# Rounding the values' weights ahead of the first keys' rotation copies, and giving the last norm's products two operands

## The chip, the cores and the metric

The kernel runs on one core of a Trainium2 chip. A core has five engines with instruction queues of their own: TensorE (PE: matmuls, and their weight loads, which the profile lists as PEld), VectorE (DVE), ScalarE (ACT), GpSimd (POOL) and SyncE (SP), which here only starts transfers. They are ordered among each other by semaphores alone. The metric is the time on the device of one execution, in microseconds (us); lower is better.

## The reference

Two layers of a transformer block over 512 tokens of width 1024, then a last norm. What matters here:

```python
def rms_norm(x, g):
    y = x * lax.rsqrt(jnp.mean(x * x, axis=-1, keepdims=True) + EPS)
    return y * g

for l in range(2):
    xn = rms_norm(x, attn_norm[l])
    (nsa_q, kv_c, kv_s, kv_w, nsa_g, cq, ckv, k_rope_raw, gate_a, gate_b) = split_cols(xn @ w_in[l])
    o_a = nsa_attention(nsa_q, kv_c, kv_s, kv_w, ...)    # rope() on queries and on the three keys
    o_b = mla_attention(cq, ckv, k_rope_raw, ...)
    merged = sigmoid(gate_a) * (o_a @ nsa_w_o[l]) + sigmoid(gate_b) * (o_b @ mla_w_o[l])
    x = x + merged @ w_out[l]
    hn = rms_norm(x, mlp_norm[l])
    x = x + jnp.square(jax.nn.relu(hn @ w_up[l])) @ w_down[l]
return rms_norm(x, final_norm)
```

## The kernel before

Activations are held transposed: `x` is 8 rows of 128 features by 512 tokens, row m being `x[:, m, :]`. Every operand of a matmul is split into a rounded part ("hi") and the rest ("lo"), and a product is three matmuls: hi by hi, hi by lo, lo by hi (lines 1375 to 1377; for the values' units 1426, 1428 and 1429). One layer is a `Fori` loop body that is written once and runs twice (l = 0 and 1).

**Weights** come in units of 128x1024 numbers (512 KB). SP loads a unit into one of two `stage` buffers, ScalarE writes its hi part (`split_hi`, line 599), and VectorE (`split_lo`, line 927) or GpSimd (`split_lo`, line 492) writes the lo part into one of two `wsplit` slots. The hi part of a unit waits for its transfer and for TensorE to have finished the unit two before it, which used the same slot. The first units of a layer are, in TensorE's order (`PREFIX`): KC (the first keys, 24 matmuls of 512 columns), VC, KS, V0 (first half of the values' unit pair, 48 matmuls of 256 columns), KW, V1, Q0, and more. GpSimd writes the lo part of V0; VectorE those of the others near it.

**Rotation** (rope) of item r, in the order of `ROPED` (KC is 0, KS is 1, KW is 2): VectorE multiplies the product tile by the cosines (`cosines`, line 977); ScalarE copies the tile with its quarters exchanged, in four instructions of 32 partitions (`swap`, line 635); VectorE multiplies that copy by the sines (line 981) and adds (line 989, both in `rotated`). What follows on ScalarE and VectorE is in written order. After KC's rotation come `copies(0)` (ScalarE, lines 670 and 671, four instructions), `blocks(0)` (VectorE, line 1009), `blocks_hi(0)` (ScalarE, line 676), and `swap(1)`. Then the hi part of V1, `rotated(1)` on VectorE, `k_hi(0)` (ScalarE, line 649, four instructions), `copies(1)`, `blocks(1)` on VectorE, `cosines(2)`, and only behind that VectorE's `split_lo` of Q0.

**ScalarE's queue** at the start of a layer: hi part of VC, `root`, hi part of KS, `spread`, `swap(0)`, hi part of V0, `copies(0)`.

**Norms.** For each row m ScalarE writes the square (line 605; row 0's goes to F[:, 2, :], the others' in turn to F[:, 1, :] and F[:, 0, :], row 7's to F[:, 1, :]) and the hi part of the scaled row (line 606). VectorE's `norm_sum` adds the square to the running sum F[:, 2, :] (line 938) and writes the lo part of the row (line 931). When all eight are added, TensorE's `mean_square` multiplies the sum by ones (line 1395: four calls, which appear as eight matmuls of one column). ScalarE takes the root (line 610), VectorE the reciprocal. There are five norms, n = 0 to 4: before layer 1, inside it, between the layers (n = 2), inside layer 2, and the last (n = 4). The sum of row 7 of norms 0 and 2 stands at the end of the work ahead of the layer's loop body, or at the end of the body.

**The end.** After the last product TensorE transposes the scaled `x` (line 1772, 32 calls of 128x128): 22 of them stand ahead of `mean_square(4)`, the others behind it. Once the reciprocal is there, ScalarE and VectorE scale the transposed tiles and SP and GpSimd send them out.

Of the kernel before, what the change touches and what calls it, by code (L numbers as in the profile page):

```python
# [12 lines left out]
P = 128  # L13
L = 2
S = 512
D = 1024
KT = D // P
QT = S // P
# [138 lines left out]
ROPED = [("KC", 0), ("KS", 0), ("KW", 0), ("Q", 0), ("Q", 1), ("Q", 2), ("Q", 3)]  # L157

PR_ATTN, PR_MLP, PR_QN, PR_KVN, PR_PE, NPAR = 0, 8, 16, 18, 19, 51
# [42 lines left out]
def build(nc, units, units_n, params, x_in, tables, cf32, cmasks, gates_dram, out):  # L202
    ctx = ExitStack()
    with ctx:
        def sb(name, shape, dt):
            return ctx.enter_context(nc.sbuf_tensor(name, shape, dt))

        def bank(name):
            return ctx.enter_context(nc.psum_tensor(name, [P, 512], F32))
# [21 lines left out]
        F = sb("F", [P, 8, S], F32)  # L231
# [7 lines left out]
        ones = sb("ones", [P, P], F32)  # L239
        par_all = sb("par_all", [P, L * NPAR + KT], F32)  # L240
        par = sb("par", [P, NPAR], F32)
        nextgain = sb("nextgain", [P, KT], F32)
# [29 lines left out]
        SB = [bank("S0"), bank("S1")]  # L272
# [4 lines left out]
        def sems(*names):  # L277
            return [sem(n) for n in names]
# [13 lines left out]
        def wslot(u):  # L292
            return narrow[:, SN[u] % 2] if u in SN else wsplit[:, BN[u] % 2]
# [81 lines left out]
        s_sq, s_sqadd = sems("s_sq", "s_sqadd")  # L375
        s_eps, s_masks, s_maskrow = sems("s_eps", "s_masks", "s_maskrow")
        s_mstand = sem("s_mstand")
        s_ms, s_rms, s_rec, s_diag, s_spread, s_rs = sems("s_ms", "s_rms", "s_rec", "s_diag", "s_spread", "s_rs")
# [217 lines left out]
        def _(act):  # L596
            def split_hi(l, u, f=0):
                split_begins(act, l, u, f)
                act.activation(wslot(u)[:, 0, :], staged(u), ACT.Copy).then_inc(s_whin if u in SN else s_whi, 1)  # L599
# [12 lines left out]
            def spread(n):  # L612
                act.wait_ge(s_spread, n + 1)
                act.activation(rs[:, :], SB[0][:, :], ACT.Copy).then_inc(s_rs, 1)
# [10 lines left out]
            with act.Fori(0, L) as l:  # L625
                def emptied(t):
                    act.wait_ge(s_gfree, l * NG + (TILE[t] + 1 + GFREE0))
# [16 lines left out]
                def k_hi(br):  # L644
                    act.wait_ge(s_roped, l * 7 + (2 + br))
                    for gr in range(2):
                        k = F[64 * gr:64 * gr + 64, 4 + (br + 1) % 2, :]
                        for hf in range(2):
                            ins = act.activation(KN[64 * hf:64 * hf + 64, br, gr, 0, :], k, ACT.Copy)
                    ins.then_inc(s_rhi, 1)  # L650

                def v_hi():
                    act.wait_ge(s_rs, l * 2 + 1)
                    act.wait_ge(s_wused, l * NU + (UNIT["V", 1] + 1 + WUSED0))
                    for tt in range(QT):
                        src = SB[tt // 2][:, 256 * (tt % 2):256 * (tt % 2) + 256].rearrange("p (a n) -> p a n", n=HD)
                        dst = VN[:, tt, :, :, 0:HD].rearrange("p b g n -> p (b g) n")
                        ins = act.activation(dst, src, ACT.Copy, scale=rc[:, 0, tt:tt + 1])
                    ins.then_inc(s_vhi, 1)

                def copies(kind):
                    if kind == 0:
                        act.wait_ge(s_roped, l * 7 + 1)
                        src = F[:, 4, :]
                    else:
                        emptied(("VC", 0))
                        act.wait_ge(s_tb, l * 2 + 1)
                        src = E[:, 0, :]
                    for gr in range(2):
                        act.activation(E[0:64, 1 + gr, :], src[64 * gr:64 * gr + 64, :], ACT.Copy)  # L670
                        ins = act.activation(E[64:128, 1 + gr, 0:S - 1], src[64 * gr:64 * gr + 64, 1:S], ACT.Copy)
                    ins.then_inc(s_cc, 1)

                def blocks_hi(kind):
                    act.wait_ge(s_tb, l * 2 + (kind + 1))
                    act.activation(TB[:, kind, :, 0, :], tbf.rearrange("p (j n) -> p j n", j=16), ACT.Copy)\
                        .then_inc(s_tbhi, 1)
# [121 lines left out]
                for u, item in enumerate(PREFIX):  # L799
                    name, i = item  # L800
                    if u in BN and item != ("GATE", FIRST_GATE - 1):
                        split_hi(l, BIG[BN[u] + 2])
                    if u == 0:
                        spread(l * 2)
                    if name == "VC":
                        copies(0)
                    if name == "KS":
                        blocks_hi(0)
                    if item == ("V", 0):
                        k_hi(0)  # L810
                        copies(1)
                    if name == "KW":
                        blocks_hi(1)
                    if item == ("V", 1):
                        v_hi()
                        k_hi(1)
                    if item == ("CQ", 0):
                        q_hi(0)
                    if item == ("CQ", 1):
                        q_hi(1)  # L820
                    if name == "CQ":
                        c_square(i)
                    if item == ("Q", 2):
                        c_root()
                    if name == "MISC":
                        q_hi(2)
                        swap_key()
                    if item == ("Q", 3):
                        nsa_gates()
                        hidden_copy(0)  # L830
                        hidden_tanh(0)
                    if item in ROPED:
                        swap(ROPED.index(item))
                    if item == ("GATE", 0):
                        hidden_hi(0)
                        split_hi(l, UNIT["W2K", 0])
                        q_hi(3)
                    if item == ("GATE", 2):
                        kc_hi()
                    if item == ("W1", 7):  # L840
                        hidden_copy(1)
                        hidden_tanh(1)
                    if name == "GATE":
                        gate_tanh(i)
                    for n in SMALL_AT.get(item, []):
                        split_hi(l, SMALL[n])
# [75 lines left out]
        def _(dve):  # L922
            chain = Chain(dve, s_dvec)

            def split_lo(l, u, f=0):
                split_rounded(dve, l, u, f)
                dve.tensor_tensor(wslot(u)[:, 1, :], staged(u), wslot(u)[:, 0, :], ALU.subtract)\  # L927
                    .then_inc(s_wlon[SN[u] % 2] if u in SN else s_wlo[BN[u] % 2], 1)

            def rest(out_ap, full, scale, hi):  # L930
                return dve.scalar_tensor_tensor(out_ap, full, scale, hi, ALU.mult, ALU.subtract)  # L931

            def norm_sum(n, m, gain):
                dve.wait_ge(s_sq, n * KT + (m + 1))
                if m > 0:
                    if m > 1:
                        dve.wait_ge(s_sqadd, n * KT + m)
                    dve.tensor_tensor(F[:, 2, :], F[:, 2, :], F[:, m % 2, :], ALU.add).then_inc(s_sqadd, 2 if m == 1 else 1)
                dve.wait_ge(s_xhi, n * KT + (m + 1))
                rest(xg[:, 1, m, :], x[:, m, :], gain, xg[:, 0, m, :]).then_inc(s_xlo, 1)  # L940

            def norm_diagonals(n):
                dve.wait_ge(s_rms, n + 1)
# [8 lines left out]
            dve.wait_ge(s_params, 16)  # L952
            split_lo(0, 0)
            for m in range(KT):
                norm_sum(0, m, par_all[:, PR_ATTN + m:PR_ATTN + m + 1])
            dve.wait_ge(s_const, 48)
            dve.tensor_copy(constb[:, :, :].rearrange("p c n -> p (c n)"), F[:, 4, 0:3 * P]).then_inc(s_masks, 1)
            with dve.Fori(0, L) as l:
# [236 lines left out]
                    dve.tensor_tensor(H[:, 1, m, :], F[:, 6 + m % 2, :], H[:, 0, m, :], ALU.subtract).then_inc(s_mglo, 1)  # L1195

                chain.restart()
                split_lo(l, 1)
                dve.wait_ge(s_xlo, l * 16 + 8)
                dve.tensor_copy(nextgain[:, :], par_all[:, bass.ds(l * NPAR + NPAR, KT)])  # L1200
# [160 lines left out]
                    up(f + 1)  # L1361
                for k in range(KT):
                    down(QUARTERS - 1, k, k < KT - 1)
                    norm_sum(l * 2 + 2, k, nextgain[:, k:k + 1])
            dve.wait_ge(s_rms, L * 2 + 1)
            dve.reciprocal(rc[:, 0, :], rc[:, 1, :]).then_inc(s_rec, 1)
            dve.wait_ge(s_rec, L * 2 + 1)
# [5 lines left out]
        def _(pe):  # L1373
# [18 lines left out]
            def mean_square(n):  # L1392
                pe.wait_ge(s_sqadd, n * KT + KT)
                for tt in range(QT):
                    ins = pe.matmul(SB[1][:, tt:tt + 1], F[:, 2, tt * P:(tt + 1) * P], ones[:, 0:1], start=True, stop=True)
                ins.then_inc(s_ms, 1)
# [371 lines left out]
            def turn_x(b, ms):  # L1768
# [4 lines left out]
                                       xs[m][:, (b % QT) * P:(b % QT) * P + P], ident)  # L1773
                return ins

            pe.wait_ge(s_gfree, L * NG + (GFREE0 - KT + 7))
            for b in range(4):
                turn_x(b, range(4)).then_inc(s_turned, 1)
            for b in range(4, 6):
                turn_x(b, range(4, 7))  # L1780
            mean_square(L * 2)
            for b in range(4, 6):
                turn_x(b, range(7, 8)).then_inc(s_turned, 1)
            pe.wait_ge(s_gfree, L * NG + GFREE0)
# [119 lines left out]
```

## Time and profile before

| what | value |
|---|---|
| median of 3 runs | 1550.94 us (1549.37 to 1550.97) |
| the profiled execution, whole | 1549.4 us |
| its span in the trace | 1547.5 us |
| PE busy | 1508.3 us, 97% of the span |
| PEld busy | 1260.6 us, 81% |
| DVE busy | 890.0 us, 58% |
| ACT busy | 723.9 us, 47% |
| POOL busy | 437.4 us, 28% |

The trace covers one execution, from its first to its last instruction; 1.9 us lie around it. A busy share says how much of the span an engine was computing. It doesn't say which engine is late at a given place: for that the waits and the timeline of a stretch are read.

### The profile page before, as it was taken

The numbers are of one execution on the slowest core, as the hardware profiler recorded it, in microseconds if no ns is written. First come the engines' busy times: TensorE is split into PE (matmuls) and PEld (weight loads), VectorE is DVE, ScalarE is ACT, GpSimd is POOL, SyncE is SP. The second block draws the span as 40 slices with busy tenths as digits, with TensorE's granted clock in tenths as the row PEclk, the third lists the DMA queues.
The fourth block names the chain that finished last, engine by engine and source line by source line (L and its number), as shares of the span: only waits on it lengthen the run. The fifth ranks groups of instructions, "written<-read, shape, count | busy, mean of one in ns | idle before, by whom it ended". The sixth has DMA issues, their size and how long they took to land.

```text
span 1547.5 us, 23290 instructions
## 1 busy us (share of the span) xinstructions
PE 1508.3 (97%) x7404; PEld 1260.6 (81%) x7404; DVE 890.0 (58%) x1537; ACT 723.9 (47%) x1316; POOL 437.4 (28%) x456
## 2 busy tenths in 40 slices
PE   6999999999999999999999999999999999999997
PEld 5888888888888888888888788787878888888886
DVE  6765755766654444535556757566675535354455
ACT  6753777874432222222366547777744212222233
POOL 1301666775010100101021036767730201010011
PEclk9999999999999999999999999999999999999999
DMA  5333212125222222322324422111352222223223
GB/s 194 109 130 123 91 67 76 42 89 173 100 95 96 95 95 95 96 95 99 105 69 136 150 82 83 56 69 57 96 176 96 96 95 96 101 94 104 95 95 109
DMA packets 43273, 155.56 MB, mean 101 GB/s; under 512 B 5312, under 2 KB 5312, under 8 KB 43168
## 3 DMA queue, kind: packets, MB, share of 16 engines
q1 hardware_dynamic: 36864, 133.19, 25.6%
q0 software_dynamic: 5728, 19.00, 3.6%
q10 hardware_dynamic: 576, 2.10, 0.4%
q8 instruction: 51, 0.84, 0.2%
q14 instruction: 54, 0.44, 0.1%
HBM read 143.78 MB, written 10.49 MB: 100 GB/s over the span
## 4 chain that ended last, share of the span: by engine, by line
PE 80%; issue 9%; DVE 3%; POOL 3%; ACT 2%; DMA 1%; POOLq 0%; DVEq 0%; ACTq 0%
PE G L1375 13%; PE G L1377 13%; PE G L1376 13%; PE O L1377 8%; PE O L1376 8%; PE O L1375 8%; PE O L1648 3%; PE T L1624 3%; PE S L1599 2%; PE T L1375 1%; PE T L1376 1%; PE T L1377 1%; POOL wsplit L492 1%; PE O L1450 1%; DVE F L1326 1%
## 5 line engine op out<-in xcount | busy, mean ns | idle before, releaser
L599 ACT ACTIVATE wsplit<-stage 128x1024 fp32r<-128x1024 f32 x229 | 242.4, 1058 | 608.9 <-PE G L1377 280.4
L927 DVE TENSOR_TENSOR wsplit<-stage,wsplit 128x1024 fp32r<-128x1024 f32 x181 | 264.3, 1460 | 70.7 <-ACT wsplit L599 64.1
L1375 PE MATMUL G<-xg,wsplit 128*128 128x512 f32 x592 | 238.6, 403 | 12.4 <-DVE xg L931 10.8
L585 POOL TENSOR_TENSOR F<-Y 128x512 f32<-128x512 f32 x64 | 68.4, 1069 | 637.3 <-DVE Y L1343 637.3
L1377 PE MATMUL G<-xg,wsplit 128*128 128x512 f32 x592 | 231.6, 391 | 0.0
L1376 PE MATMUL G<-xg,wsplit 128*128 128x512 f32 x592 | 231.6, 391 | 0.0
L492 POOL TENSOR_TENSOR wsplit<-stage,wsplit 128x1024 fp32r<-128x1024 f32 x48 | 116.1, 2419 | 138.3 <-ACT wsplit L599 137.8
L1134 DVE CUSTOM_DVE_ANT_0 F<-S,F 128x512 f32<-128x512 f32 x192 | 93.7, 488 | 101.6 <-PE S L1599 64.4
L1375 PEld LDWEIGHTS G<-xg,wsplit 128*128 128x128 f32 x592 | 111.6, 189 | 37.2 <-DVE xg L931 13.8
L754 ACT ACTIVATE F<-F,nmx 128x512 f32<-128x512 f32 x192 | 107.7, 561 | 64.9 <-DVE nmx L1134 63.1
L1377 PEld LDWEIGHTS G<-xg,wsplit 128*128 128x128 f32 x592 | 111.4, 188 | 24.4
L1376 PEld LDWEIGHTS G<-xg,wsplit 128*128 128x128 f32 x592 | 111.7, 189 | 20.7 <-issue 1.0
L1375 PE MATMUL G<-area,wsplit 128*128 128x512 f32 x320 | 124.7, 390 | 0.1
L1375 PE MATMUL O<-area,wsplit 128*128 128x512 f32 x320 | 124.5, 389 | 0.0
L1376 PE MATMUL G<-area,wsplit 128*128 128x512 f32 x320 | 124.5, 389 | 0.0
L1377 PE MATMUL O<-area,wsplit 128*128 128x512 f32 x320 | 124.5, 389 | 0.0
L1377 PE MATMUL G<-area,wsplit 128*128 128x512 f32 x320 | 124.5, 389 | 0.0
L1376 PE MATMUL O<-area,wsplit 128*128 128x512 f32 x320 | 124.5, 389 | 0.0
L1144 DVE TENSOR_TENSOR area_b<-T,area_b 128x512 fp32r<-128x512 f32 x192 | 92.8, 483 | 25.1 <-ACT area_b L749 22.3
L1375 PE MATMUL O<-xg,wsplit 128*128 128x512 f32 x256 | 99.6, 389 | 0.0
L1376 PE MATMUL O<-xg,wsplit 128*128 128x512 f32 x256 | 99.6, 389 | 0.0
L1377 PE MATMUL O<-xg,wsplit 128*128 128x512 f32 x256 | 99.6, 389 | 0.0
(286 smaller groups left out, 3001.9 us busy)
## 6 DMA issues: line engine op xcount, KB each, us to landing
stage<-units SPq DMA_DIRECT2D x230, 512.0 KB, 3.3
stage_n<-units_n SPq DMA_DIRECT2D x22, 512.0 KB, 3.3
gates<-Y POOLq DMA_DIRECT2D x32, 256.0 KB, 2.7
E<-gates POOLq DMA_DIRECT2D x24, 256.0 KB, 3.7
x<-x_in ACTq DMA_DIRECT2D x4, 512.0 KB, 7.1
F<-gates POOLq DMA_DIRECT2D x8, 256.0 KB, 3.8
rope<-tables POOLq DMA_DIRECT2D x1, 768.0 KB, 7.1
out<-F SPq DMA_DIRECT2D x3, 256.0 KB, 2.2
```

The costliest lines, as they stand in the source:

```text
L492: pool.tensor_tensor(wslot(u)[:, 1, :], staged(u), wslot(u)[:, 0, :], ALU.subtract)\
L585: pool.tensor_tensor(F[:, m % 2, :], Y[:, m % 2, :], Y[:, m % 2, :], ALU.mult)\
L599: act.activation(wslot(u)[:, 0, :], staged(u), ACT.Copy).then_inc(s_whin if u in SN else s_whi, 1)
L754: act.activation(prob(i, w), prob(i, w), ACT.Exp, bias=nmx[:, i % 4:i % 4 + 1], scale=-1.0, accum_out=sums[:, i % 4:i % 4 + 1]).then_inc(s ...
L927: dve.tensor_tensor(wslot(u)[:, 1, :], staged(u), wslot(u)[:, 0, :], ALU.subtract)\
L1134: dve.tensor_tensor_reduce(prob(i, w), score_tile(i), maskrow[:, S - w:S], -1.0, 1e38, ALU.add, ALU.min, nmx[:, i % 4:i % 4 + 1]).then_inc ...
L1144: dve.tensor_tensor(pt_view(slot, 1, qt), tp_view(j % 2, qt), pt_view(slot, 0, qt), ALU.subtract)\
L1375: pe.matmul(dst, a(0), b(0), start=first, stop=False)
L1376: pe.matmul(dst, a(0), b(1), start=False, stop=False)
L1377: return pe.matmul(dst, a(1), b(0), start=False, stop=last)
L1624: ins = pe.transpose(TP[j % 2][:, kt * P:(kt + 1) * P], prob(j, S)[:, kt * P:(kt + 1) * P], ident)
L1648: ins = pe.matmul(dst[:, kt * P:S], v, PT[:, slot, c, kt * S:(kt + 1) * S - kt * P], start=opens and c == 0, stop=closes(j) is not None an ...
```

## The change

Three edits. ScalarE's `swap(0)` moves from its place ahead of V0's hi part to the place right behind it. The running sum's last addition is taken out of `norm_sum`: for norms 0 and 2 it becomes the first instruction of the layer's body on VectorE, ahead of the lo part of VC and behind the lo part of row 7. For norm 4 the addition is dropped, and TensorE multiplies two operands by ones and accumulates them: the sum of seven rows, and the last row's square. Norms 1 and 3 keep `norm_sum` as it was.

```diff
 (ScalarE, in the loop over PREFIX)
                     if name == "VC":
+                        swap(0)
                         copies(0)
...
-                    if item in ROPED:
+                    if item in ROPED and u > 0:
                         swap(ROPED.index(item))
 (VectorE)
-            def norm_sum(n, m, gain):
+            def row_sum(n, m):
                 dve.wait_ge(s_sq, n * KT + (m + 1))
                 if m > 0:
                     if m > 1:
                         dve.wait_ge(s_sqadd, n * KT + m)
                     dve.tensor_tensor(F[:, 2, :], F[:, 2, :], F[:, m % 2, :], ALU.add).then_inc(s_sqadd, 2 if m == 1 else 1)
+
+            def row_lo(n, m, gain):
                 dve.wait_ge(s_xhi, n * KT + (m + 1))
                 rest(xg[:, 1, m, :], x[:, m, :], gain, xg[:, 0, m, :]).then_inc(s_xlo, 1)
+
+            def norm_sum(n, m, gain):
+                row_sum(n, m)
+                row_lo(n, m, gain)
...
             for m in range(KT):
-                norm_sum(0, m, par_all[:, PR_ATTN + m:PR_ATTN + m + 1])
+                if m < KT - 1:
+                    row_sum(0, m)
+                row_lo(0, m, par_all[:, PR_ATTN + m:PR_ATTN + m + 1])
...
                 chain.restart()
+                row_sum(l * 2, KT - 1)
                 split_lo(l, 1)
...
                     down(QUARTERS - 1, k, k < KT - 1)
-                    norm_sum(l * 2 + 2, k, nextgain[:, k:k + 1])
+                    if k < KT - 1:
+                        row_sum(l * 2 + 2, k)
+                    row_lo(l * 2 + 2, k, nextgain[:, k:k + 1])
 (TensorE, at the end)
+            def last_squares(src, first):
+                for tt in range(QT):
+                    ins = pe.matmul(SB[1][:, tt:tt + 1], src[:, tt * P:(tt + 1) * P], ones[:, 0:1],
+                                    start=first and tt == 0, stop=not first, skip_group_check=True)
+                return ins
...
                 turn_x(b, range(4, 7))
-            mean_square(L * 2)
+            pe.wait_ge(s_sqadd, L * 2 * KT + KT - 1)
+            last_squares(F[:, 2, :], True)
+            pe.wait_ge(s_sq, L * 2 * KT + KT)
+            last_squares(F[:, 1, :], False).then_inc(s_ms, 1)
             for b in range(4, 6):
```

## Rows read from the trace of the kernel before

**Rows 1.** Page, chain of work that ended last, shares by engine and line.
```profile
PE 80%; issue 9%; DVE 3%; POOL 3%; ACT 2%; DMA 1%; POOLq 0%; DVEq 0%; ACTq 0%
```
**Rows 2.** Waits of TensorE, whole span: total us, times, longest.
```profile
PE S L1426 <- POOL wsplit L492: 3.0, 2, 1.5
```
**Rows 3.** Timeline of TensorE, first 52 us: start, us, line, tiles, idle before.
```profile
26.38 0.39 PE L1377 MATMUL G<-xg,wsplit 128*128 128x512 f32 x1
...
33.70 0.36 PE L1426 MATMUL S<-wsplit,xg 128*128 128x256 f32 x1 [1.49 <-POOL wsplit L492]
...
51.38 0.49 PE L1375 MATMUL G<-xg,wsplit 128*128 128x512 f32 x1 [0.48 <-DVE wsplit L927]
```
**Rows 4.** Timeline of ScalarE, 27 to 46 us.
```profile
27.48 2.40 ACT L635 ACTIVATE F<-G 32x512 f32<-32x512 f32 x4 [2.16 <-DVE F L977]
29.90 1.06 ACT L599 ACTIVATE wsplit<-stage 128x1024 fp32r<-128x1024 f32 x1
31.36 0.63 ACT L670 ACTIVATE E<-F 64x512 f32<-64x512 f32 x1 [0.40 <-DVE F L989]
...
37.04 2.40 ACT L635 ACTIVATE F<-T 32x512 f32<-32x512 f32 x4
39.73 1.07 ACT L599 ACTIVATE wsplit<-stage 128x1024 fp32r<-128x1024 f32 x1 [0.29 <-PE S L1429]
40.91 2.56 ACT L649 ACTIVATE area<-F 64x512 fp32r<-64x512 f32 x4
...
45.43 0.63 ACT L671 ACTIVATE E<-E 64x511 f32<-64x511 f32 x1
```
**Rows 5.** Timeline of VectorE, 26 to 52 us.
```profile
26.75 0.69 DVE L977 TENSOR_TENSOR F<-G,Y 128x512 f32<-128x512 f32 x1
...
30.63 0.69 DVE L989 TENSOR_TENSOR F<-F 128x512 f32<-128x512 f32 x1
...
40.19 0.69 DVE L989 TENSOR_TENSOR F<-F 128x512 f32<-128x512 f32 x1
...
47.05 2.00 DVE L1009 TENSOR_TENSOR E<-E,par 128x496 f32<-128x496 f32 x1
...
49.57 1.68 DVE L927 TENSOR_TENSOR wsplit<-stage,wsplit 128x1024 fp32r<-128x1024 f32 x1
```
**Rows 6.** Timeline of GpSimd, the lo part of V0 in layer 1.
```profile
31.04 2.51 POOL L492 TENSOR_TENSOR wsplit<-stage,wsplit 128x1024 fp32r<-128x1024 f32 x1 [21.20 <-ACT wsplit L599]
```
**Rows 7.** Timeline of VectorE, row 7 of norm 0 and entry into layer 1.
```profile
17.09 0.68 DVE L938 TENSOR_TENSOR F<-F 128x512 f32<-128x512 f32 x1
17.69 0.75 DVE L931 SCALAR_TENSOR_TENSOR xg<-x,par_all,xg 128x512 fp32r<-128x512 f32 x1
...
18.62 1.22 DVE L927 TENSOR_TENSOR wsplit<-stage,wsplit 128x1024 fp32r<-128x1024 f32 x1
```
**Rows 8.** Timeline of TensorE, KC and the first matmul of VC, layer 1.
```profile
11.09 0.63 PE L1375 MATMUL G<-xg,wsplit 128*128 128x512 f32 x1
...
18.49 0.50 PE L1375 MATMUL G<-xg,wsplit 128*128 128x512 f32 x1 [0.30 <-DVE xg L931]
...
20.12 0.49 PE L1375 MATMUL G<-xg,wsplit 128*128 128x512 f32 x1
```
**Rows 9.** Timelines of VectorE and TensorE where layer 2 begins.
```profile
778.94 1.23 DVE L927 TENSOR_TENSOR wsplit<-stage,wsplit 128x1024 fp32r<-128x1024 f32 x1 [2.46 <-ACT wsplit L599]
...
780.29 0.49 PE L1375 MATMUL G<-xg,wsplit 128*128 128x512 f32 x1 [0.45 <-DVE wsplit L927]
```
**Rows 10.** DMA queues in 775 to 779.5 us: packets, MB, share.
```profile
q14 instruction: 4, 0.03, 2.6%
```
**Rows 11.** Timelines of VectorE, TensorE and ScalarE at the last norm.
```profile
1536.24 0.69 DVE L938 TENSOR_TENSOR F<-F 128x512 f32<-128x512 f32 x1 [0.78 <-ACT F L605]
...
1536.99 1.05 PE L1395 MATMUL S<-ones,F 128*128 128x1 f32 x8
...
1538.08 0.26 ACT L610 ACTIVATE rc<-S,small 128x4 f32<-128x4 f32 x1 [1.26 <-PE S L1395]
```

## The prediction on record

> **What bounds the kernel now.** I read the chain of work that ended last first. TensorE makes up 80% of it [rows 1], so a microsecond is won or lost only where TensorE stands idle, or at the two ends of the kernel. Next I read TensorE's waits. The wait for GpSimd's lo part of V0 appears twice, once a layer, 3.0 us in total [rows 2]: that is the wait which the moved `swap(0)` bears on. Then I read the timelines of the stretch, engine by engine, to see what comes late once that wait is gone. TensorE stands idle 1.49 us before V0, then works without a gap, and stands idle once more, 0.48 us, before Q0's first matmul at 51.38 [rows 3]. The reader should note that this second wait ends with VectorE's lo part of Q0, and ask what that in turn hangs on.
>
> It hangs on a chain through ScalarE and VectorE that begins with `swap(0)`. Link by link: cosines(0) end at 26.75 + 0.69 = 27.44 [rows 5]; swap(0) starts at 27.48 and ends at 29.88 [rows 4]; the two instructions of rotated(0) end at 30.63 + 0.69 = 31.32 [rows 5]; copies(0) start at 31.36, behind an idle 0.40 that this addition ends, and not V0's hi part, which was done at 29.90 + 1.06 = 30.96 [rows 4]. Copies, blocks(0), blocks_hi(0) and swap(1) follow. swap(1) runs from 37.04 to 39.44 [rows 4]. rotated(1) ends at 40.19 + 0.69 = 40.88 [rows 5] and k_hi(0) starts at 40.91, although ScalarE was free at 39.73 + 1.07 = 40.80 [rows 4]: the rotation was the later of the two. copies(1) end at 45.43 + 0.63 = 46.06 [rows 4]; blocks(1), stretched by a 2.00 us instruction, end at 49.05, cosines(2) follow, and the lo part of Q0 ends at 49.57 + 1.68 = 51.25 [rows 5]. TensorE starts at 51.38. Not one of these links waits for TensorE or for V0. A delay of swap(0) arrives whole at Q0.
>
> **The change, part one: swap(0) behind V0's hi part.** V0's hi part needs VC finished on TensorE: last matmul at 26.38 + 0.39 = 26.77 [rows 3]. With one semaphore's lag of about 0.04 (27.44 to 27.48 above) it starts at 26.81. It takes 1.06 and the next instruction follows 0.03 later: swap(0) starts at 27.90 instead of 27.48, **0.42 us late**. V0's lo part follows at 27.96 instead of 31.04 [rows 6] and ends near 30.4, ahead of the 32.21 (33.70 less 1.49) at which TensorE had finished KS. So the 1.49 us wait goes. But Q0 now starts 0.42 later than before, since its chain starts 0.42 later; the 1.49 us gained before V0 is spent waiting at Q0, where the idle grows from 0.48 to 0.48 + 1.49 + 0.42 = 2.4 us, or some 2.2 us and the rest before KW, whose lo part also moves back by 0.42. Behind Q0 all three engines are later by the same 0.42 and keep their distances. Layer 2 shows the same two waits in the same order, so I count it the same: 2 x 0.42 = **+0.84 us**. The bounds: nothing at all lost if a link has slack that I don't see (lower end 0), and 0.42 plus 0.15 a layer if rotated(0), starting at 30.33 while GpSimd still works on V0, is held up by it (upper end 1.14). I take 0.84, because every link shows its start within 0.04 us of the end before it.
>
> V0's transfer is no hindrance: SP can start it when VC's lo part is done (18.62 + 1.22 = 19.84 [rows 7]), seven microseconds ahead. SP's next transfer, V1's, starts about 3 us sooner, and nobody waited for it.
>
> **Part two: row 7's addition moved, norm 0.** VectorE now does the lo part of row 7 in place of the addition, at 17.09 and not 17.69 [rows 7], then the constants' cast, then the addition. TensorE's last three matmuls of KC waited for that lo part, 0.30 us at 18.49 [rows 8]. They start earlier, and mean_square with them. The next limit is the lo part of VC: the same instructions stand ahead of it in sum, so it still ends at 19.84, and VC can begin about 0.12 later (778.94 + 1.23 = 780.17, start 780.29 [rows 9]), at 19.96 in place of 20.12 [rows 8]. **-0.16 us.** Bounds: 0, and -0.30 if the whole wait were to come back.
>
> **Part two again, norm 2, where layer 2 begins.** Here the lo part of row 7 didn't wait for the addition but for ScalarE, so nothing comes earlier. The addition now stands behind the loop's jump, ahead of VC's lo part, and TensorE waited for just that lo part: 0.45 us at 780.29 [rows 9]. An addition takes 0.69 alone and 0.60 in a row of instructions (17.09 to 17.69 [rows 7]). The question is whether it fits into VectorE's idle 2.46 us before 778.94. The row names ScalarE's hi part as the releaser, but that unit's hi part began 1.6 us after ScalarE's own last work, and VectorE started 0.58 us after it ended, where 0.04 is usual. So VectorE itself wasn't back from the jump before 778.94, and the instruction queue's transfers run in this stretch [rows 10]. The addition then runs at about 778.94 and everything behind it is 0.61 later: **+0.61 us**, with bounds 0 (it fits into the idle time) and 0.8 (its two waits are worked out behind the jump too). The Trainium skill has a rule for this, in "Runtime: NRT & Kernel Launch", section "Instruction fetch mechanics": a taken branch to a page that isn't held makes the engine wait for a fetch before it goes on. By that rule the addition can't use the gap and costs its 0.6; by the releaser that the profile names it would cost nothing.
>
> **Part three, the last norm.** The addition of row 7 ends at 1536.24 + 0.69 = 1536.93, and the eight one-column matmuls begin at 1536.99 [rows 11]. Its removal looks like 0.69 us won. But TensorE was transposing without a gap up to 1536.98: no idle stands in front of that row. At most 0.12 us, the distance of one weight load, is won. What is added is a second set of eight. A set takes 1.05 us from first start to last end, with a last matmul of about 0.27, so (1.05 - 0.27) / 7 = 0.11 apart, 0.92 for eight. The first set isn't ready-made in idle time either; it stands behind the same transposes. So the root, released by the last of them at 1538.08 [rows 11], comes 0.92 - 0.12 = **+0.80 us** later, and behind it the reciprocal, the scaling and the output transfers, with nothing else to hide it. Bounds: 0.4, if the second set's loads overlap better, and 0.95.
>
> **Sum.** 0.84 - 0.16 + 0.61 + 0.80 = +2.1 us. The profiled execution took 1549.4 whole (span 1547.5 and 1.9 around it), so 1551.5 by it. The median shown is 1.54 above that execution: **1553.0 us**. The bounds add up to 0 - 0.30 + 0 + 0.4 = +0.1 and 1.14 + 0 + 0.8 + 0.95 = +2.9. The difference that a measurement of this kernel can tell from none is about 0.2%, 3.1 us. The forecast is 0.14% slower, inside it: no change.
>
> **Rivals.**
> *The wait at V0 is really won.* If a link of the chain to Q0 has slack of 2 us, both waits shrink: 2 x -1.49 - 0.16 + 0.61 + 0.80 = -1.7, 1549.2 us. For it speaks that this is the longest wait of the stretch; against it each link in rows 4 and 5. Chance 0.08.
> *The addition fits into the gap at the jump.* +1.5 in all, 1552.4 us. For it speaks the releaser in rows 9; against it the 0.58 us lag. Chance 0.15.
> *The longer idle time costs TensorE its clock; this one ends slower.* In the kernel's first matmuls, after 9.6 us of idleness, a matmul of 512 columns takes 0.63 [rows 8] against 0.39 later [rows 3], which are the levels of 1.2 and 2.4 GHz. After 1.49 us of idleness the clock was still at 2.4 GHz. The idle time before Q0 grows to 2.2 to 2.4 us, between the two. If the clock falls there, the price by the kernel's start, where about six matmuls went slow, is 6 x 0.24 = 1.4 us a layer: 2.1 + 2.8 = +4.9, 1555.8 us, 0.3% slower. It decides if as few as three matmuls go slow in each layer (0.7 a layer, 3.5 in all). "TensorE: Matmul & The Clock Gate", Part 1, in the Trainium skill says that idleness brings the lower clock back; no row here shows an idle time of this length, so it stays open which side of that rule it falls on. Chance 0.12.
> The forecast itself has 0.65.
>
> **How the numbers follow.** Faster by over 0.2% would need more than the first rival gives: 0.04, half of its chance, for unseen slack on top. Slower by over 0.2%: the clock's 0.12 and 0.04 for a sum at its upper end: 0.16. Within 0.2%: 0.80. The range runs from 1550.5, which holds the bound of +0.1 less the scatter of the three runs shown, to 1555.5, which leaves out the far half of the clock's case; the first rival lies outside it. The forecast's own range is 1551.0 to 1554.0.
>
> **What the profile of the changed kernel would show.** Right: no wait before V0; swap(0) starting 1.09 us behind the start of V0's hi part and 1.1 us behind the end of VC's last matmul; a wait of 2.2 us or more before Q0, still ended by VectorE's lo part; Q0 at about 51.38 - 0.16 + 0.42 = 51.64; at the layer's start an addition on VectorE at about 778.9 with 0.6 us more before VC; 16 one-column matmuls at the end and the root 0.8 us later, counted from the last product. Wrong: Q0 starting earlier than 51.2, matmuls of 0.63 us behind its wait, or the 16 taking no longer than the eight did.

## The result and the profile after

The changed kernel takes **1553.56 us** in the median of 11 executions (1550.27 to 1556.02), the kernel before 1550.36 in its 11 (1549.15 to 1552.08). The ratio is 1.002, with a 95% interval of 1.001 to 1.0029: slower by 0.2%, some 3 us. The forecast was 1553.0 us in 1550.5 to 1555.5, and 0.14% slower. The second measurement of the same kernel (e13 below) gives 1.0021 (1.0012 to 1.003).

The profiled execution took 1555.03 us, with a span of 1553.2. That is 5.7 us above the span of before, and nearly twice what the medians differ by, so it can't be read as the price of the change before it is taken apart. First come TensorE's waits over the whole span (total us, times, longest us), with those left out that hardly moved:

```profile
PE G L1387 <- DVE wsplit L928: 4.6, 4, 2.2
...
PE S L1407 <- DVE F L939: 0.7, 1, 0.7
...
PE T L1387 <- DVE wsplit L928: 0.3, 2, 0.2
```

The wait for V0 [rows 2] is gone, and the waits for VectorE's lo parts took its place: two of 2.1 to 2.2 us before Q0, and two of 0.16 before KW (two of 0.16 before VC are in the first row as well). A new one, for the moved addition, stands where layer 2 begins. The timelines of layer 1 show the chain, beginning with TensorE (the first row is VC, the second KW, the third Q0):

```profile
20.07 0.50 PE L1387 MATMUL G<-xg,wsplit 128*128 128x512 f32 x1 [0.16 <-DVE wsplit L928]
...
38.06 0.51 PE L1387 MATMUL T<-xg,wsplit 128*128 128x512 f32 x1 [0.16 <-DVE wsplit L928]
...
51.70 0.49 PE L1387 MATMUL G<-xg,wsplit 128*128 128x512 f32 x1 [2.12 <-DVE wsplit L928]
```

ScalarE and VectorE in the same stretch:

```profile
26.75 1.06 ACT L599 ACTIVATE wsplit<-stage 128x1024 fp32r<-128x1024 f32 x1 [1.49 <-PE G L1389]
27.84 2.39 ACT L635 ACTIVATE F<-G 32x512 f32<-32x512 f32 x4
31.71 0.63 ACT L670 ACTIVATE E<-F 64x512 f32<-64x512 f32 x1 [1.48 <-DVE F L998]
...
41.27 2.56 ACT L649 ACTIVATE area<-F 64x512 fp32r<-64x512 f32 x4 [0.40 <-DVE F L998]
```
```profile
49.93 1.65 DVE L928 TENSOR_TENSOR wsplit<-stage,wsplit 128x1024 fp32r<-128x1024 f32 x1
```

Counted from VC's first matmul, which takes out what differs ahead of it, swap(0) starts 7.77 us later where it was 7.36 [rows 4, 8], and Q0 31.63 us later where it was 31.26 [rows 3, 8]. The delay of 0.41 passes down the links (copies(0) 0.40, k_hi(0) 0.41, the lo part of Q0 0.41) and is 0.37 at TensorE. V0's earlier start is all in the wait.

Where layer 2 begins, first row 7's lo part on VectorE in the kernel before, then VectorE and TensorE in the changed kernel:

```profile
775.72 0.75 DVE L931 SCALAR_TENSOR_TENSOR xg<-x,nextgain,xg 128x512 fp32r<-128x512 f32 x1
```
```profile
778.84 0.75 DVE L932 SCALAR_TENSOR_TENSOR xg<-x,nextgain,xg 128x512 fp32r<-128x512 f32 x1 [1.39 <-ACT xg L606]
782.19 0.69 DVE L939 TENSOR_TENSOR F<-F 128x512 f32<-128x512 f32 x1 [2.59 <-issue]
782.80 1.22 DVE L928 TENSOR_TENSOR wsplit<-stage,wsplit 128x1024 fp32r<-128x1024 f32 x1
```
```profile
782.94 1.05 PE L1407 MATMUL S<-ones,F 128*128 128x1 f32 x8 [0.73 <-DVE F L939]
784.15 0.49 PE L1387 MATMUL G<-xg,wsplit 128*128 128x512 f32 x1 [0.16 <-DVE wsplit L928]
784.48 0.39 PE L1388 MATMUL G<-xg,wsplit 128*128 128x512 f32 x1
784.71 0.46 PE L1389 MATMUL G<-xg,wsplit 128*128 128x512 f32 x1
784.97 0.63 PE L1387 MATMUL G<-xg,wsplit 128*128 128x512 f32 x1
```

The addition waits out the jump as well: its idle time of 2.59 us is now put down to "issue" and to no other engine, where in [rows 9] the profile had named ScalarE. The square that it adds had been written at 778.19, so it had nothing else to wait for. Then comes something that no price of the forecast's sum holds. From 784.97 on a matmul takes 0.63 us instead of 0.39: TensorE's clock has fallen from 2.4 to 1.2 GHz (the granted clock from 785 to 788 us is 0.50). Eight matmuls later it is back. They took 3.4 us where eight at the usual distance of 0.23 take 1.84, so this fall costs 1.5. There is another in this execution, near 88 us, that begins within the 24 one-column matmuls of the latent norms:

```profile
86.43 3.15 PE L1529 MATMUL T<-ones,csq 128*128 128x1 f32 x24
...
91.29 0.63 PE L1387 MATMUL T<-xg,wsplit 128*128 128x512 f32 x1
```

The busy times of 88 to 92 us (PE, PEld, DVE, ACT, POOL; then the granted clock, the DMA share, GB/s) give 0.57 for the clock:

```profile
88.00:92.00 4.00, 4.00 (x21) 3.90 (x21) 0.94 (x1) 2.33 (x6) 0.00 (x0) 0.57 0.04 14
```

The last norm: the last product in the kernel before, then TensorE and ScalarE in the changed kernel:

```profile
1534.35 0.39 PE L1377 MATMUL O<-area,wsplit 128*128 128x512 f32 x1
```
```profile
1539.26 0.39 PE L1389 MATMUL O<-area,wsplit 128*128 128x512 f32 x1
...
1541.89 1.84 PE L1790 MATMUL S<-ones,F 128*128 128x1 f32 x16
```
```profile
1543.77 0.26 ACT L610 ACTIVATE rc<-S,small 128x4 f32<-128x4 f32 x1 [2.04 <-PE S L1790]
```

From the last product's start to the root it is 4.51 us. Before it was 1538.08 less 1534.35, 3.73 us: 0.78 more.

**How executions are compared below.** Each execution lists its mean granted clock. In the kernel before it takes values from 0.995 to 0.998, and the time goes with it: the 92 executions in the first three rows of the table below average 1552.2, 1550.4, 1549.3 and 1548.4 us at 0.995, 0.996, 0.997 and 0.998. So beside the medians I compare executions with the same mean clock, as long as the kernels end alike (the clock also falls behind the last matmul, and a kernel with another end shifts the mean by that). The changed kernel ends a little otherwise: its clock is low for the last 7.1 us of its profile and 6.8 of e13's, against 5.8 before. That lowers its mean by 0.0003 to 0.0004, so a difference at equal clock is good to some 0.4 us there.

### The profile page after: what moved, and what is told of

The parts are those of the page before. It is cut to its first block, busy times and chain, and to the rows that moved or that the text cites. A ratio compares the mean times of both kernels' runs of the same rounds, so it can differ in the third digit from the quotient of the medians.

```text
span 1553.2 us, 23306 instructions
## 1 busy us (share of the span) xinstructions
PE 1512.6 (97%) x7412; PEld 1265.1 (81%) x7412; DVE 888.5 (57%) x1536; ACT 723.9 (47%) x1316; POOL 437.1 (28%) x456
## 4 chain that ended last, share of the span: by engine, by line
PE 83%; issue 5%; DVE 5%; ACT 3%; POOL 3%; DMA 1%; DVEq 0%; POOLq 0%; ACTq 0%
PE G L1387 14%; PE G L1389 13%; PE G L1388 13%; PE O L1389 8%; PE O L1388 8%; PE O L1387 8%; PE O L1660 3%; PE T L1636 3%; PE S L1611 2%; PE T L1387 2%; PE T L1389 1%; PE T L1388 1%; POOL wsplit L492 1%; PE O L1462 1%; ACT F L635 1%
```

## The experiments

| kernel | median us (n) | ratio, 95% | mean us at clock 0.998 (n) | executions at 0.995 or less |
|---|---|---|---|---|
| before, beside e1 to e4 | 1550.39 (33) | | 1548.5 (8) | 1 |
| before, beside e6 to e10 | 1549.98 (27) | | 1548.3 (7) | 1 |
| before, beside e11 to e14 | 1550.21 (32) | | 1548.4 (2) | 0 |
| changed | 1553.56 (11) | 1.002, 1.001 to 1.0029 | 1550.3 (1) | 4 |
| changed again, e13 | 1553.34 (11) | 1.0021, 1.0012 to 1.003 | 1550.8 (3) | 4 |
| e1, swap(0) moved | 1552.11 (11) | 1.0014, 1.0004 to 1.0023 | 1549.4 (3) | 5 |
| e14, e1 with the wait filled | 1550.55 (11) | 1.0002, 0.9993 to 1.0011 | 1549.1 (3) | 1 |
| e2, additions moved | 1551.78 (11) | 1.0015, 1.0006 to 1.0024 | 1550.7 (3) | 4 |
| e3, two operands at the end | 1551.08 (11) | 1.0007, 0.9998 to 1.0017 | 1549.5 (1) | 2 |
| e4, swap moved, Q0 early | 1549.84 (11) | 0.9998, 0.9989 to 1.0007 | none | 1 |
| e6, two operands, early | 1549.85 (11) | 1.0001, 0.9992 to 1.001 | ends otherwise | 1 |
| e8, squares spread | 1550.95 (11) | 1.0008, 0.9999 to 1.0018 | 1550.9 (7) | 0 |
| e9, changed, squares spread | 1556.42 (5) | 1.0042, 1.0028 to 1.0056 | none | 3 |
| e10, e4, e6 and e8 together | 1549.67 (11) | 1.0001, 0.9992 to 1.001 | ends otherwise | 0 |
| e11, e4 and e6 together | 1549.13 (11) | 0.9993, 0.9984 to 1.0002 | ends otherwise | 0 |
| e12, e11 and CQ0 early | 1546.33 (10) | 0.9977, 0.9968 to 0.9987 | ends otherwise | 0 |

### The parts one by one: e1, e2, e3

**e1** is the kernel before with the diff's two edits of `swap` and nothing else.

> Only ScalarE's swap(0) is moved behind V0's hi part; the norms are as in the kernel before. Theory (the chain from swap(0) to Q0's lo part has no slack): no wait before V0, a wait of 2.1 to 2.4 us before Q0, Q0's first matmul 0.4 us later than before in both layers, 0.8 us slower in all (ratio about 1.0005, same). Rival (the wait at V0 is really won): 3 us faster, ratio 0.998. Rival (the longer idle time before Q0 costs TensorE its clock): matmuls of 0.63 us right behind that wait, 1.4 us a layer more, ratio about 1.002. Second rival on the clock, from the changed kernel's trace: it falls elsewhere, at the start of layer 2, and then this kernel shows no slow matmuls there, because it has no added wait at that place.

Its profiled execution shows the waits of layer 1 that the theory names, and no slow matmuls behind them:

```profile
PE G L1376 <- DVE wsplit L928: 2.1, 1, 2.1
...
PE T L1376 <- DVE wsplit L928: 0.2, 1, 0.2
```

At a mean clock of 0.998 it takes 1549.4 against 1548.5 us, 0.9 us more; the forecast's term was 0.84. The rival in which V0's wait is really won falls. But the median is 1.7 us up, and 5 of 11 executions have a clock of 0.995 or less, where the kernel before has 2 in 92. The rival on the clock isn't refuted by a single profile without a fall.

**e2** moves the additions of norms 0 and 2; that of norm 4 stands behind the loop:

```diff
+                row_sum(l * 2, KT - 1)
                 split_lo(l, 1)
...
+            row_sum(L * 2, KT - 1)
             dve.wait_ge(s_rms, L * 2 + 1)
```

> Only the additions of row 7 of norms 0 and 2 are moved to the start of the layer's body; that of norm 4 stands behind the loop, and the last products are as before. Theory: 0.1 to 0.2 us earlier in layer 1, 0.6 us later in layer 2, 0.45 us slower in all. If the clock falls at the start of layer 2 because of the wait that this edit adds ahead of the one-column matmuls, eight matmuls of 0.63 us or so follow in the first tile of layer 2 and cost 1.6 us more: about 2 us slower, ratio 1.0013. Rival (the fall is chance or belongs to another edit): none of them here, ratio 1.0003.

It came out 2.2 us slower at equal clock (three executions; 1.4 in the median) and not 0.45. Two things that its forecast didn't price show in its profile. The first is its own end, TensorE and then VectorE:

```profile
1539.42 1.05 PE L1407 MATMUL S<-ones,F 128*128 128x1 f32 x8 [1.12 <-DVE F L938]
```
```profile
1538.01 0.75 DVE L931 SCALAR_TENSOR_TENSOR xg<-x,nextgain,xg 128x512 fp32r<-128x512 f32 x1 [1.39 <-ACT xg L606]
1538.68 0.68 DVE L938 TENSOR_TENSOR F<-F 128x512 f32<-128x512 f32 x1
```

The addition now stands behind row 7's lo part, which waits for ScalarE's hi part. VectorE shows no idle time at the loop's exit; the written order alone makes the addition late, and TensorE waits 1.12 us for it. The root comes 5.01 us behind the last product's start (1535.50 to 1540.51), where it was 3.73: 1.28 more. The second is the start of layer 2: from the start of row 7's lo part to VC's first matmul it is 5.52 us (776.80 to 782.32) against 4.57 (775.72 to 780.29), 0.95 more, of which 0.34 is a longer jump (VectorE idle 2.80 us where it was 2.46). With 0.15 won at norm 0, 1.28 + 0.95 - 0.15 makes 2.1 of the 2.2.

No fall of the clock stood at the start of layer 2 in its profile, though the same wait of 0.7 us did. So the fall at that place isn't certain in any one execution. And 4 of its 11 executions are at 0.995 or less although Q0's wait is as it was: the low executions don't come from that wait alone.

What the addition costs at the jump is read from the profiles: the same stretch is 5.31 us in the changed kernel and 5.33 in e13, 0.74 and 0.76 more than before. In e1, which doesn't touch this place, it is 4.89, because the jump took 0.3 longer there.

**e3** takes the two operands at the end alone. Row 7's sum goes into a row of its own, so that the sum of seven rows is still there for norm 4:

```diff
-                    dve.tensor_tensor(F[:, 2, :], F[:, 2, :], F[:, m % 2, :], ALU.add).then_inc(s_sqadd, 2 if m == 1 else 1)
+                    dve.tensor_tensor(F[:, 3 if apart else 2, :], F[:, 2, :], F[:, m % 2, :], ALU.add).then_inc(s_sqadd, 2 if m == 1 else 1)
...
-            mean_square(L * 2)
+            pe.wait_ge(s_sqadd, L * 2 * KT + KT - 1)
+            last_squares(F[:, 2, :], True)
+            pe.wait_ge(s_sq, L * 2 * KT + KT)
+            last_squares(F[:, 1, :], False).then_inc(s_ms, 1)
```

> Only the last norm takes two operands, at the same place in TensorE's queue as in the changed kernel. Row 7 of norms 0, 2 and 4 is still added where it was, but into a row of its own, which the products of norms 0 and 2 read. Theory: 16 one-column matmuls instead of 8, the root 0.8 us later counted from the last product, 0.8 us slower in all, nothing else changed. Rival (the addition that is gone from the path counts): 0 to 0.6 us faster.

The 16 matmuls take 1.84 us and the root comes 4.51 us behind the last product's start, as in the changed kernel: 0.78 more than before. The median is 0.7 us up, in an interval that just holds no change. The theory held in the profile, and the median fits it without telling it from no change.

### Is Q0's chain what swallows the gain: e4, e12

**e4** takes Q0's parts out of the chain's end:

```diff
                         k_hi(0)
+                        split_hi(l, UNIT["Q", 0])
                         copies(1)
...
                     if item == ("V", 0):
+                        split_lo(l, UNIT["Q", 0])
                         blocks(1)
```

> swap(0) moved as in e1, and Q0's hi part taken ahead of copies(1) on ScalarE, its lo part ahead of blocks(1) on VectorE. Theory (the 1.49 us won at V0 are lost at Q0 alone): both waits vanish, Q0 starts near 49.7 us instead of 51.4, about 1.7 to 1.9 us faster a layer as long as the tiles behind Q0 aren't late (they carry 1.1 us more of ScalarE's work ahead of them), 2 to 3.6 us faster in all, ratio 0.998. Rival (something else than Q0's weights holds TensorE there): no faster than the kernel before.

Half right. Q0's wait vanished, but a new one came a unit later, before CQ0:

```profile
56.48 0.49 PE L1378 MATMUL G<-xg,wsplit 128*128 128x512 f32 x1 [1.54 <-DVE wsplit L929]
```

Of up to 3.6 us it kept a few tenths: its executions at a clock of 0.997 average 1549.1, those of the kernel before beside them 1549.9 (two only), and all 18 of the kernel before 1549.3. So Q0's weights were what held TensorE, and behind them stand CQ0's.

**e12** is e11 (below) with CQ0's parts moved forward in the same way.

```diff
                     if name == "KW":
+                        split_hi(l, UNIT["CQ", 0])
                         blocks_hi(1)
...
+                        split_lo(l, UNIT["CQ", 0])
                         blocks_lo(1)
```

> e11 with the same treatment of the next unit: CQ0's hi part ahead of blocks_hi(1) on ScalarE, its lo part ahead of blocks_lo(1) on VectorE. Theory (the time won at V0 travels to the first unit whose parts are late, and is kept once none is): the wait of 1.5 us before CQ0, which took Q0's place in e4, goes too, and Q1 is ready in time: up to 1.5 us a layer faster than e11, 3 to 4 us under the kernel before, ratio 0.9975 to 0.998. Rival (the wait only moves one unit further, to Q1 or later): within 0.5 us of e11.

It is the one kernel clearly faster than before: 1546.33 us, ratio 0.9977 (0.9968 to 0.9987), and 2.8 us below e11. Q0 starts at 49.58 us, in a row with V1, where it started at 51.38 [rows 3], and two units on only 0.19 us of waiting is left:

```profile
49.58 0.40 PE L1380 MATMUL G<-xg,wsplit 128*128 128x512 f32 x1
...
60.84 0.49 PE L1380 MATMUL T<-xg,wsplit 128*128 128x512 f32 x1 [0.19 <-DVE wsplit L930]
```

The time won at V0 is real once no unit behind it is late. No run moves Q0's and CQ0's parts without `swap(0)`; the waits that those moves alone could take away in the kernel before are 0.48 us in layer 1 [rows 3] and 0.51 in layer 2, well under the 2.8 us of the step from e11 to e12.

### The end in another order: e6, e11

**e6** puts the seven rows' products ahead of all transposes and the last square's behind eight of them:

```diff
+            last_squares(F[:, 2, :], True)
+            for b in range(2):
+                turn_x(b, range(4)).then_inc(s_turned, 1)
+            pe.wait_ge(s_sq, L * 2 * KT + KT)
+            last_squares(F[:, 1, :], False).then_inc(s_ms, 1)
+            for b in range(2, 4):
```

> The two operands of the last norm as in e3, but in another place of TensorE's queue: the products of the seven rows' sum stand ahead of all transposes, those of the last square behind eight of them, and the other 14 transposes that stood ahead follow behind. Theory (the two operands cost time only because TensorE reaches them late): the last square is there 1.5 us after the last product, the root comes 0.6 to 0.8 us earlier than before counted from the last product, 0.6 to 0.8 us faster in all. Rival (the transposes left behind then hold the scaling up, or the added products count wherever they stand): no faster than the kernel before.

```profile
1536.15 1.02 PE L1778 MATMUL S<-ones,F 128*128 128x1 f32 x8
```
```profile
1537.21 0.26 ACT L610 ACTIVATE rc<-S,small 128x4 f32<-128x4 f32 x1 [0.53 <-PE S L1778]
```

The last product starts at 1534.21 here, so the root is 3.00 us behind it: 0.73 earlier than before, and the span ends 12.5 us behind it instead of 13.15. Its two fastest executions, 1547.52 and 1547.66, lie 0.5 and 0.4 us below the fastest of the 27 beside them (1548.03). The median, 1549.85 against 1549.98, doesn't tell it from no change.

**e11** joins e4 and e6.

> e4 and e6 together: swap(0) behind V0's hi part, Q0's parts early, the last norm's products ahead of the transposes; the latent norms' squares stand where they stood. If the savings add at equal clock: 1.1 us under the kernel before (0.4 by e4, 0.7 by e6). Rival: no better than e4 alone.

1549.13 us, 1.1 below the kernel before beside it, as added up, but its interval (0.9984 to 1.0002) reaches to no change.

### The clock: e8, e9, e14, e13

**e8** has nothing of the change. It issues the 24 one-column matmuls between those of Q2's tile.

```diff
-                        project(item)
-                    if item == ("Q", 2):
-                        c_mean_squares()
+                        project(item, c_mean_squares if item == ("Q", 2) else None)
```

> The kernel before, with nothing of the change. The 24 one-column matmuls of the latent norms, which stand in a row near 87 us of each layer, are issued between the matmuls of Q2's tile, six ahead of each of its last four k steps. Theory (the lower clock near 88 to 96 us and its twin in layer 2, seen in some executions, comes from that row of one-column matmuls): no fall of the clock at either place, all executions at a mean granted clock of 0.998, 1 to 2 us faster in the median and a much smaller scatter. Rival (the falls are chance, wherever they land): the same scatter and the same mean clock of 0.996 to 0.997.

The clock part held: all 11 executions at 0.998 or 0.999, and times within 0.8 us (1550.65 to 1551.44) where 27 of the kernel before spread over 4. The time didn't come back. Q2's tile ends later, and with it the rotation ahead of the latent norms' diagonals; TensorE waits 1.74 us for them in each layer, instead of 0.54 in layer 1:

```profile
97.01 1.98 PE L1528 MATMUL G<-csq,ones 128*128 128x512 f32 x4 [1.74 <-DVE csq L1037]
```

**e9** is the changed kernel with the same spreading.

> The changed kernel with the 24 one-column matmuls spread as in e8. Theory (the change costs about 2 us by its chain and the rest of its excess is lower clock at places that both kernels have or that its added wait at the start of layer 2 makes): 1550.5 us where the mean clock is 0.998, that is 2 us above e8, and lower clock only at the start of layer 2 in some executions. Rival (the longer idle time before Q0 brings the clock down in some executions): executions at 0.996 or less remain often, and slow matmuls right behind Q0's wait.

My 1550.5 us left out what e8 costs, which I didn't know when I wrote it. What counts is its profile, of an execution at 0.995. The clock falls right behind the long wait before Q0, ahead of the edit's own place, and again in layer 2, at 816.76, behind a wait of 2.17 us that ends at 815.90:

```profile
51.53 0.49 PE L1387 MATMUL G<-xg,wsplit 128*128 128x512 f32 x1 [2.14 <-DVE wsplit L928]
51.86 0.50 PE L1388 MATMUL G<-xg,wsplit 128*128 128x512 f32 x1
52.16 0.63 PE L1389 MATMUL G<-xg,wsplit 128*128 128x512 f32 x1
52.59 0.63 PE L1387 MATMUL G<-xg,wsplit 128*128 128x512 f32 x1
```

So the forecast's third rival exists: in this execution the clock falls right behind both waits before Q0, in the profiled ones of the changed kernel, e1 and e13, with waits of 2.12 to 2.17 us at the same places, it doesn't.

**e14** tests it on e1, with work in that wait:

```diff
+                        if item == ("Q", 0):
+                            free(item)
+                            for k in range(8):
+                                pe.matmul(g_tile(item)[:, :], xg[:, 0, k, 0:P], xg[:, 0, k, :], start=True, stop=True)
                         project(item)
```

> e1 with work for TensorE in the wait before Q0: eight matmuls of 512 columns whose product is overwritten by Q0's own. They leave out nothing of the computation. Theory (the long idle time before Q0 lowers the clock in some executions): the wait shrinks to about 0.3 us, Q0 starts when it did in e1, and executions at a mean clock of 0.995 or less become as rare as in the kernel before (2 of 60, against 5 of 11 in e1); median 0.8 to 1.0 us above the kernel before. Rival (e1's low executions have another cause): as many of them as in e1, median 1.7 us above.

```profile
49.39 2.00 PE L1586 MATMUL G<-xg 128*128 128x512 f32 x8
51.63 0.50 PE L1376 MATMUL G<-xg,wsplit 128*128 128x512 f32 x1 [0.23 <-DVE wsplit L928]
```

Q0 starts when it did in e1 (51.62), and with the useless matmuls the median is 1550.55 us against e1's 1552.11. The two were measured beside different executions of the kernel before; against these e14 is 0.3 us slower and e1 1.7, and their intervals overlap (0.9993 to 1.0011, and 1.0004 to 1.0023). One execution of 11 is at 0.995, none below; e1 had five. With 11 executions each, chance alone would part them so far in some 7% of cases. Both have 0.7 to 0.9 us over the kernel before at a clock of 0.998. It speaks for the wait as the cause of e1's low executions, and doesn't prove it.

**e13** measured the changed kernel again.

> The changed kernel once more, beside executions of the kernel before on the same chip. Theory: where both have a mean granted clock of 0.998, 1.8 to 2.3 us slower than before; in the median 2.5 to 3.5 us slower, the rest being a lower clock in more of its executions. Rival (it is all in the instructions): the same difference at equal clock as in the median.

At 0.998 its three executions average 1550.8 us. Together with the one of the first measurement (1550.27) that is 1550.7, against 1548.4 for the 17 of the kernel before: 2.3 us. Beside its own executions of the kernel before e13 alone has 2.4. The medians differ by 3.1.

**e10** was meant as the best version, with e4, e6 and e8 together.

> swap(0) behind V0's hi part, Q0's parts early as in e4, the last norm as in e6, the squares as in e8. If the three savings add at equal clock (0.4 by e4, 0.7 by e6, and what the clock gives back, 1 to 2), it takes 1547 to 1548 us, 2 to 3 us under the kernel before, ratio 0.998 to 0.9987. Rival (they get in each other's way, since all work through VectorE's and ScalarE's queues in the same 100 us): no better than the best of its parts.

1549.67 us: the wait that e8 makes is in it (1.74 us before the diagonals), and the wait before CQ0 (1.56). All executions lie within 0.8 us, but it isn't faster than the kernel before.

## Why the prediction was right

**V0's wait goes and Q0's grows: right, and shown.** Forecast 0.42 us a layer; 0.37 in layer 1 by the profile, 0.39 in layer 2 (VC's to Q0's first matmul 781.23 to 812.88 in e13, 31.65 us, against 780.29 to 811.55), 0.9 us for e1 at equal clock against 0.84. The waits came to 2.12 and 0.16 where the text had 2.2 and the rest. e4 and e12 show the cause by removing it. That rotated(0) might be held up by GpSimd, the upper bound, didn't show.

**Norm 0: right.** VC starts 10.33 us behind KC's first matmul (9.74 to 20.07), before 10.48 (9.64 to 20.12): 0.15 less, forecast 0.16. It is ended by VC's lo part, as said.

**Norm 2: right.** The addition ran behind the jump, and the profile's releaser in [rows 9] was misleading, as argued from the lag of 0.58 us. The Trainium skill, "Runtime: NRT & Kernel Launch", section "Instruction fetch mechanics", says that a taken branch to a page of instructions that isn't held makes the engine wait for a fetch. The trace agrees: an idle time of 2.59 us with no other engine to blame, and 2.62 in e13. The stretch grew by 0.74 to 0.76 where I had 0.61. From the first instruction behind the jump to VC's first matmul it is 1.96 us (782.19 to 784.15) against 1.35 (778.94 to 780.29): 0.61, the term itself. The other 0.13 to 0.15 is the jump, 2.59 and 2.62 against 2.46. Over the profiles it averages 2.57 in the ten without an addition behind it (2.46 to 2.78) and 2.73 in the four with one (2.59 to 2.89); whether the addition lengthens it stays open.

**The last norm: right, and luckier than it looks.** 0.78 us, forecast 0.80, in the changed kernel and in e3. The addition was not on the path; TensorE's own queue was. But two slips cancel in the 0.80. The 0.12 that the removal should have won wasn't: the one-column matmuls start 2.63 us behind the last product's start (1539.26 to 1541.89), where it was 2.64 (1534.35 to 1536.99). And the second set costs 1.84 - 1.05 = 0.79, not 0.92; eight at the forecast's own distance of (1.05 - 0.27) / 7 make 0.89.

**The sum: 2.1 forecast.** The pieces read from profiles make 0.37 + 0.39 - 0.15 + 0.74 + 0.78 = 2.1, and at equal clock it is 2.3. The remaining 0.9 us of the median's 3.2 goes with a lower clock. Here the forecast was too sure. It gave 0.12 to the case that the long idle time costs TensorE its clock, and thought of it as happening in every execution or in none. In fact the clock falls in some: 8 of the changed kernel's 22 executions are at 0.995 or less, 2 of the 92 of the kernel before. It also falls at a place that I hadn't looked at, the start of layer 2. In which share of the executions each of these places falls stays open; the profiles show one execution each. Of the forecast's signs of being wrong, matmuls of 0.63 us behind Q0's wait stand in neither profile of the changed kernel, but in e9's. The Trainium skill, "TensorE: Matmul & The Clock Gate", Part 1, says that idleness brings the lower clock back. e9's profile agrees (0.63 us a matmul behind 2.14 and 2.17 us of idleness); those of the changed kernel, e1 and e13 show idle times as long and no fall behind them. The rival's price was also too high: it took 0.24 us a slow matmul, the difference of the durations, where their starts lie 0.42 to 0.43 apart (784.97 to 785.39) instead of 0.23, so 0.2.

That the median came within 0.6 us of 1553.0 is in part luck. The forecast started from the median of three executions, 1550.94, which is 0.6 above the median of eleven, 1550.36; this hides half of the 1.1 us by which the difference of the medians exceeds the forecast's 2.1.

**The bookkeeping of the profiled execution.** Of its 5.7 us, 3.1 are there where layer 1 ends (row 7's lo part at 778.84 instead of 775.72). It is 0.3 after Q0; the fall near 88 us adds 2.5 (from the first of the 24 matmuls to the products with the latent norms' diagonals it is 12.28 us, 86.43 to 98.71; before 9.81, 86.13 to 95.94). At the start of layer 2 the fall adds 1.5 and the addition 0.7, and Q0's chain 0.4 behind it. Near 848 us it is the profile before that has a fall, which takes 0.7 off again. At the last product's start it is 4.9, at the root 5.7. A reader who had taken 5.7 us for the change's price would have been wrong by a factor of more than two.

## What to carry to other kernels

A wait that is taken away ahead of one unit is only won if no unit behind it is late: follow the chain to the next wait of the engine that bounds, and see whether anything in it hangs on the one removed. If not, the gain waits there, and the next unit's work has to be moved too, until none is late (here two units on: e12 is 3.9 us below the kernel before, some 0.7 of it by its other end). At a place where the bounding engine works without a gap, taking work off another engine and giving it some costs time, however long the other's instruction was; put it where the engine's next work has slack. And where executions of one kernel scatter by 4 us, compare those of equal clock before reading a microsecond out of a median.

## What the runs showed of the hardware

- TensorE's clock fell to 1.2 GHz for two to nine matmuls of 512 columns, at a cost of 1.5 us for the eight at 784.97, in some executions and not in others. It did so in or behind three kinds of work: 24 one-column matmuls in a row (88 and 848 us; in one layer at least in 9 of the 11 profiles that have them, the kernel before among them), eight of them with waits of 0.73 and 0.16 us around (the changed kernel's profile, not e13's or e2's), and idle times of 2.14 and 2.17 us (e9's profile, not those of the changed kernel, e1 and e13). With the 24 spread among full matmuls no fall stands there in the three profiles (e8, e9, e10), and e8's 11 executions are all at 0.998 or 0.999.
- VectorE came back from the layer loop's jump 2.46 to 2.89 us after its last instruction ended, in 14 profiles. At the loop's exit e2's profile shows no idle time on it.
